# Depthwise convolution: the last terms of each channel tile as matrix products with diagonals

## The chip, the cores and the metric

The kernel runs on one core of one Trainium2 chip. Its time is the device time of one execution in microseconds (us). Three executions of the kernel before took 3126.61, 3127.12 and 3130.42 us; the median, 3127.12, is the time before. The engines are PE (TensorE, the matrix engine), DVE (VectorE), ACT (ScalarE), POOL (GpSimd) and SP (SyncE, which here issues the weight transfers). SBUF is the on-chip memory that all of them read, PSUM the memory into which PE writes its sums, in eight banks of 512 float32 for each of 128 partitions.

## The reference, cut to what matters

Two blocks run one after the other on 256 tokens of width 1024, all in float32. The second block also carries 256 context tokens, so its first layer works on 512 columns. In that first layer, between two feed-forward parts, stands the module that the change touches:

```
def conformer_conv(h, pw1_w, pw1_b, dw_w, dw_b, ln_g, ln_b, pw2_w, pw2_b):
    a = h @ pw1_w + pw1_b
    u, g = jnp.split(a, 2, axis=-1)
    u = u * jax.nn.sigmoid(g)
    u = lax.conv_general_dilated(            # depthwise, width 31, centred
        u, dw_w[:, None, :], window_strides=(1,), padding=[(15, 15)],
        feature_group_count=D_MODEL) + dw_b
    mu = jnp.mean(u, axis=-1, keepdims=True)
    var = jnp.mean(jnp.square(u - mu), axis=-1, keepdims=True)
    u = (u - mu) * lax.rsqrt(var + NORM_EPS) * ln_g + ln_b
    return jax.nn.silu(u) @ pw2_w + pw2_b
```

It is applied to the latent tokens and to the context tokens apart. The second layer has an attention in its place. Each layer is steered by nine vectors (shift, scale and gate of three parts), `silu(c) @ ada_w + ada_b`: a product of two rows with a matrix of 1024 x 9216.

## The kernel before, in words

**Layout.** Channels lie on the partitions, 128 at a time: KT = 8 channel tiles. Tokens lie along the free dimension. In the second block's first layer a tile is 512 columns: two sequences of 256.

**Split products.** A float32 product is made of three fast ones. Both operands are split into a high part (rounded by ACT in a copy) and a low part (the rest, by DVE or POOL: `low = raw - high`). `mm3` multiplies low by high, high by low and high by high into one sum.

**The stream of weights.** All weights stand in HBM in the order of their use, cut into quarters of 128 x 512 float32 (256 KB). `stream()` lists them. SP loads them in that order into a ring of RING = 11 places (`raw`). A place is free again when the quarter 11 before has been split (its low part is done) or, for an unsplit quarter, when PE has used it. ACT makes the high parts (`high`, L1277), and mostly DVE the low parts (`low`, L1720).

**Fills.** The steering products are done in 36 "fills" strewn over the kernel: one fill is eight unsplit quarters, multiplied with the two rows `cs` (`ps<-raw,cs`, 16 instructions on PE). Afterwards ACT copies the result (`row_buf`), PE turns it into columns (`ps<-cst,row_buf`) at the start of the next fill, and DVE takes the columns (`mods_raw`, then `mods` and `mod_a`). 18 fills stand in the conv stage: two for each channel tile and two behind. LATE_FILLS = 3 stand in the attention of the second layer, between its projections and its scores, in front of one more that PE does behind the scores.

**The conv stage** (`conv` of each engine). For channel tile n, PE computes the two halves of the first pointwise product into the banks 2(n%2) and 2(n%2)+1: four quarters, in two halves of 24 matmuls, with a fill behind each. ACT takes the sigmoid of one bank (`gated<-ps,cst`), and DVE multiplies and writes the result to `conv_in` (`hidden<-ps,cst,gated`: "the gate"; `conv_in`, `conv_out` and `side` are all pieces of the buffer `hidden` and bear its name in the trace). PE may write a pair of banks again when the gate two tiles before is done.

Then come the 31 terms. A term is `sum = conv_in[shifted by t] * w[t] + sum` over 128 x 512, one instruction (scalar_tensor_tensor, L1723). Each waits for the one before (`link`), since it reads its sum. DVE keeps the running sum `acc` in PSUM, bank 4 + n%2; only the last term writes to `conv_out` in SBUF. The first SIDES[n] terms of tile n = 1 to 7 are not done by DVE: ACT multiplies (`hidden<-hidden,cst` on ACT, into one of four buffers `side`) and POOL adds them up in `conv_out` (L2304 for the first, L2306 for the others). DVE waits for their sum and starts from it, so its first term of such a tile reads `conv_in` and `conv_out` and writes PSUM (`ps<-hidden,cst`), its middle ones read `conv_in` and PSUM (`ps<-hidden,cst,ps`), and the last reads the same and writes `conv_out` (`hidden<-hidden,cst,ps`).

The order within each engine is written out by hand. DVE takes the gate of tile n+2 near the end of tile n. POOL makes the low parts of the weight quarters from tile 1 on (L2276), two of them between the first side sums of each tile and two at its end. ACT makes the high parts at fixed places between its side products.

When all eight tiles are summed, PE forms the mean, DVE subtracts it, PE forms the variance, and norm, silu and the second pointwise product follow.

## Time and profile before

| | before |
|---|---|
| device time, median of 3 | 3127.12 us (3126.61 to 3130.42) |
| span of the profiled execution, first to last instruction | 3127.4 us |
| PE busy | 2965.4 us, 95% |
| DVE busy | 1637.2 us, 52% |
| ACT busy | 1291.8 us, 41% |
| POOL busy | 167.0 us, 5% |
| weights moved | 443.10 MB in all, 142 GB/s over the span |

The span of the profiled execution and the times of the others agree to 0.1%. Shares are means over stages with different limits. The profile also cuts the span into 40 slices of 78 us and gives the busy share of each engine in tenths:

```profile
PE   7999899999998999999999878999999999989998
DVE  5565765555647656533335796433335333448554
ACT  4444445455544455432332444323324323335553
POOL 0000010000010100000000670000000000000000
```

The conv stage is where POOL has its 6 and 7. Names such as `ps<-hidden,cst,ps` say what an instruction writes and reads: `ps` is PSUM, `hidden` and all others are SBUF. `cst` holds constants, here the weight w[t] of a term, one value for each partition. 128x512 is partitions times elements. The text in brackets at the end of a row is the idle time of the engine before it, and who ended it.

### The profile page before, as it was taken

The numbers are of one execution on the slowest core, as the hardware profiler recorded it, in microseconds if no ns is written. First come the engines' busy times: TensorE is split into PE (matmuls) and PEld (weight loads), VectorE is DVE, ScalarE is ACT, GpSimd is POOL, SyncE is SP. The second block draws the span as 40 slices with busy tenths as digits, with TensorE's granted clock in tenths as the row PEclk, the third lists the DMA queues.
The fourth block names the chain that finished last, engine by engine and source line by source line (L and its number), as shares of the span: only waits on it lengthen the run. The fifth ranks groups of instructions, "written<-read, shape, count | busy, mean of one in ns | idle before, by whom it ended". The sixth has DMA issues, their size and how long they took to land.

```text
span 3127.4 us, 51125 instructions
## 1 busy us (share of the span) xinstructions
PE 2965.4 (95%) x17586; PEld 2533.1 (81%) x17586; DVE 1637.2 (52%) x3043; ACT 1291.8 (41%) x2519; POOL 167.0 (5%) x121
## 2 busy tenths in 40 slices
PE   7999899999998999999999878999999999989998
PEld 7978789799797897788886545788878888768998
DVE  5565765555647656533335796433335333448554
ACT  4444445455544455432332444323324323335553
POOL 0000010000010100000000670000000000000000
PEclk9999899999998999999999988999999999989999
DMA  7555265555652656533333762333314233241553
GB/s 256 184 163 199 72 202 178 174 183 182 181 161 69 220 179 177 172 108 95 104 97 114 256 223 81 121 95 96 105 54 139 92 106 98 81 143 50 175 181 98
DMA packets 239052, 443.10 MB, mean 142 GB/s; under 512 B 26400, under 2 KB 27424, under 8 KB 238240
## 3 DMA queue, kind: packets, MB, share of 16 engines
q1 hardware_dynamic: 237344, 432.94, 44.1%
q0 software_dynamic: 1536, 7.86, 0.8%
q8 instruction: 108, 1.77, 0.2%
q14 instruction: 64, 0.52, 0.1%
HBM read 439.65 MB, written 1.05 MB: 141 GB/s over the span
## 4 chain that ended last, share of the span: by engine, by line
PE 82%; DVE 12%; issue 2%; POOL 2%; ACT 1%; DMA 1%; SPq 0%; DVEq 0%; POOLq 0%; ACTq 0%
PE ps L736 81%; DVE low L1720 1%; DVE hidden L1723 1%; POOL hidden L2306 1%; DVE zl L1723 1%; DMA raw<-weights 1%; DVE ps L1723 1%; DVE hidden L1720 1%; DVE zl L1720 1%; DVE coef L2228 1%; DVE hidden L2232 1%; POOL low L2276 1%; DVE gated L1720 1%; DVE hidden L2055 0%; DVE neg_max L2028 0%
## 5 line engine op out<-in xcount | busy, mean ns | idle before, releaser
L736 PE MATMUL ps<-zh,low 128*128 128x256 f32 (+1 forms) x4192 | 1400.6, 334 | 79.1 <-DVE low L1720 41.1
L736 PE MATMUL ps<-zl,high 128*128 128x256 f32 (+1 forms) x4192 | 1381.8, 330 | 0.0
L736 PE MATMUL ps<-zh,high 128*128 128x256 f32 (+1 forms) x4192 | 1380.9, 329 | 0.0
L1720 DVE TENSOR_TENSOR low<-raw,high 128x512 fp32r<-128x512 f32 x1276 | 843.8, 699 | 462.1 <-ACT high L1277 460.3
L1277 ACT ACTIVATE high<-raw 128x512 fp32r<-128x512 f32 x1304 | 761.7, 625 | 572.6 <-PE ps L736 499.5
L736 PEld LDWEIGHTS ps<-zh,low 128*128 128x128 f32 x4192 | 806.0, 192 | 184.0 <-DVE low L1720 42.2
L736 PEld LDWEIGHTS ps<-zl,high 128*128 128x128 f32 x4192 | 806.7, 192 | 71.8 <-issue 4.8
L736 PEld LDWEIGHTS ps<-zh,high 128*128 128x128 f32 x4192 | 806.5, 192 | 69.1
L1720 DVE TENSOR_TENSOR hidden<-gated,ps 128x256 f32 (+1 forms) x176 | 91.5, 520 | 604.2 <-ACT gated L1277 604.2
L1277 ACT ACTIVATE gated<-ps 128x256 f32<-128x256 f32 (+1 forms) x176 | 81.3, 462 | 497.3 <-PE ps L736 497.1
L736 PE MATMUL ps<-high,zl 128*128 128x512 f32 (+2 forms) x544 | 195.2, 359 | 3.8 <-DVE zl L1720 3.8
L736 PE MATMUL ps<-low,zh 128*128 128x512 f32 (+2 forms) x544 | 195.0, 359 | 0.0
L736 PE MATMUL ps<-high,zh 128*128 128x512 f32 (+2 forms) x544 | 195.0, 358 | 0.0
L1723 DVE SCALAR_TENSOR_TENSOR ps<-hidden,cst,ps 128x512 f32<-128x512 f32 x167 | 126.1, 755 | 5.4
L736 PEld LDWEIGHTS ps<-high,zl 128*128 128x128 f32 x544 | 103.1, 189 | 19.4 <-DVE zl L1720 4.3
L736 PEld LDWEIGHTS ps<-high,zh 128*128 128x128 f32 x544 | 103.2, 190 | 15.2
L736 PEld LDWEIGHTS ps<-low,zh 128*128 128x128 f32 x544 | 103.2, 190 | 15.1
L1277 ACT ACT_TABLE_LOAD x61 | 78.3, 1283 | 84.8 <-PE ps L736 83.0
L1277 ACT ACTIVATE zh<-hidden 128x256 fp32r<-128x256 f32 (+1 forms) x190 | 94.6, 506 | 45.0 <-DVE hidden L1720 28.4
L1720 DVE TENSOR_TENSOR zl<-hidden,zh 128x256 fp32r<-128x256 f32 (+1 forms) x190 | 101.3, 545 | 2.0 <-ACT zh L1277 1.9
L1723 DVE SCALAR_TENSOR_TENSOR x<-ps,mods,x 128x256 f32<-128x256 f32 x80 | 35.0, 479 | 126.3 <-PE ps L736 126.3
L1277 ACT ACTIVATE hidden<-ps,neg_max 128x128 f32<-128x128 f32 (+2 forms) x128 | 61.5, 484 | 81.0 <-DVE neg_max L2028 49.3
(190 smaller groups left out, 2016.8 us busy)
## 6 DMA issues: line engine op xcount, KB each, us to landing
raw<-weights SPq DMA_DIRECT2D x1640, 256.0 KB, 3.4
hidden<-norms POOLq DMA_DIRECT2D x4, 1024.0 KB, 7.0
cst<-consts SPq DMA_DIRECT2D x1, 1829.0 KB, 14.3
x<-x_in SPq DMA_DIRECT2D x1, 1024.0 KB, 7.0
x<-tokens_in POOLq DMA_DIRECT2D x1, 1024.0 KB, 13.8
x<-ctx_in POOLq DMA_DIRECT2D x1, 1024.0 KB, 6.4
out<-hidden POOLq DMA_DIRECT2D x1, 1024.0 KB, 5.1
ple_p<-p_in POOLq DMA_DIRECT2D x1, 512.0 KB, 7.2
```

Source lines behind the costliest of these rows:

```text
L736: return nc.tensor.matmul(out, lhsT, rhs, start=first, stop=last, **kw)
L1277: return nc.scalar.activation(out, in_, func, **kw)
L1720: return nc.vector.tensor_tensor(out, a, b, op)
L1723: return nc.vector.scalar_tensor_tensor(out, a, s, b, op0, op1)
L2228: self.link(nc.vector.tensor_reduce(coef[:, j, 0:1], ps[:, score_bank(j), :], AX.X, ALU.max))
L2232: nc.vector.tensor_copy(probs_t[:, b, :], ps[:, 3 + b, :]).then_inc(probs_t_ready, 1)
L2276: nc.gpsimd.tensor_tensor(r(low[:, q % RING, :]), raw[:, q % RING, :], high[:, q % RING, :], ALU.subtract).then_inc(low_ready, 1)
L2306: nc.gpsimd.tensor_tensor(part, part, side[:, at % 4, :], ALU.add).then_inc(side_added, 1)
```

## The change

- The last 4 terms of the tiles 0 to 6 and the last 12 of tile 7 (TAP_QUARTERS) are done by PE. For each term the weight is a 128 x 128 diagonal matrix; four of them make a quarter, and ten such quarters are added to the stream. ACT makes the high and POOL the low part, as of other weights. `tap_product` multiplies them with shifted views of a window of `conv_in`: `window_of` on ACT writes its high part, `window_of` on DVE its low part, into a buffer `split_buf` that is also the old `h_split`. The sum stands in bank 4 + n%2, and DVE adds it (`add_taps`), which ends a tile.
- DVE's running sum moves from PSUM to `conv_out` in SBUF for all its terms.
- SIDES shrinks from (0, 7, 9, 9, 9, 9, 9, 13) to (0, 3, 6, 7, 7, 7, 7, 4): 41 instead of 65 terms by way of ACT and POOL.
- The eight quarters of tiles 0 and 1 have no fill between them, and DVE makes their low parts ahead of the stage. The conv stage has 15 fills instead of 18, and LATE_FILLS is 6 instead of 3.
- POOL makes the low parts from tile 2 on and those of the ten diagonal quarters: 34 instead of 28.
- The gate of tile n+1 is taken in the middle of tile n instead of the gate of n+2 near its end.

```diff
-SIDES = (0, 7, 9, 9, 9, 9, 9, 13)
-LATE_FILLS = 3
+SIDES = (0, 3, 6, 7, 7, 7, 7, 4)
+TAP_QUARTERS = (1, 1, 1, 1, 1, 1, 1, 3)
+LATE_FILLS = 6
+WINDOW = 268
+def conv_fill(n, a):
+    return n >= 2 or (n, a) == (1, 1)
+def taps_by_pe(n):
+    return 4 * TAP_QUARTERS[n]
@@ stream, the conv part
             for t in range(KT):
                 for a in range(2):
                     yield ("up_half", ("conv", 0), (t, a), 2, False)
-                    yield fills.pop()
-            yield fills.pop()
-            yield fills.pop()
+                    if conv_fill(t, a):
+                        yield fills.pop()
+                if t >= 2:
+                    yield ("taps", ("conv", 0), t - 2, TAP_QUARTERS[t - 2], False)
+            for t in (KT - 2, KT - 1):
+                yield ("taps", ("conv", 0), t, TAP_QUARTERS[t], False)
+                yield fills.pop()
@@ class PE
+            def tap_product(self, n, z0):
+                self.pe.wait_ge(tap_low, n + 1)
+                if n >= 2:
+                    self.pe.wait_ge(z_ready, z0 + n - 1)
+                last = taps_by_pe(n) - 1
+                for c0 in range(0, last, 4):
+                    h, lo = self.quarter()
+                    for i in range(4):
+                        at = slice(c0 + i, c0 + i + S)
+                        w = (h[:, i * P:i * P + P], lo[:, i * P:i * P + P])
+                        m = self.mm3(ps[:, 4 + n % 2, :], w, (window[:, n % 2, 0, :, at], window[:, n % 2, 1, :, at]), c0 + i == 0, c0 + i == last)
+                    self.done(m)
@@ class PE, conv
                     for a in range(2):
...
-                        self.fill(6, 7)
+                        if conv_fill(n, a):
+                            self.fill(6, 7)
+                    if n >= 2:
+                        self.tap_product(n - 2, z0)
                 seen(conv_taken, KT)
-                self.fill(6, 7)
-                self.fill(6, 7)
+                for n in (KT - 2, KT - 1):
+                    self.tap_product(n, z0)
+                    self.fill(6, 7)
@@ class Act
+            def window_of(self, n):
+                self.act.wait_ge(conv_taken, self.seen.now(conv_taken) + n + 1)
...
+                self.f(r(window[:, n % 2, 0, :, 0:wide]), conv_in[:, n, :, at:at + wide], ACT.Copy).then_inc(tap_high, 1)
@@ class Act, conv, at the end of a tile's side products
                     if n < KT - 1:
-                        self.q += 2
                         self.gate_of(n + 1)
-                        self.fill(6, 7)
-                    if n < KT - 2:
+                        filled()
                         self.next_high()
                         self.next_high()
+                        self.take_rows()
+                        self.window_of(n + 1)
@@ class Dve, conv
+                def window_of(n):
+                    wide, at = S + taps_by_pe(n) - 1, TAPS - taps_by_pe(n)
+                    v.wait_ge(tap_high, n + 1)
+                    self.tt(r(window[:, n % 2, 1, :, 0:wide]), conv_in[:, n, :, at:at + wide], window[:, n % 2, 0, :, 0:wide], ALU.subtract).then_inc(tap_low, 1)
+                def add_taps(n):
+                    v.wait_ge(quarter_done, taps_at[n] + TAP_QUARTERS[n] + RING)
+                    self.tt(conv_out[:, n, :], conv_out[:, n, :], ps[:, 4 + n % 2, :], ALU.add).then_inc(z_ready, 1)
                 for n in range(KT):
-                    acc = ps[:, 4 + n % 2, :].rearrange("p (a s) -> p a s", a=2)
                     part = conv_out[:, n, :].rearrange("p (a s) -> p a s", a=2)
-                    for t in range(first, TAPS):
-                        last = t == TAPS - 1
-                        i = self.stt(part if last else acc, conv_in[:, n, :, t:t + S], w[:, n, t:t + 1], part if n and t == first else acc, ALU.mult, ALU.add)
...
+                    for t in range(first, last + 1):
+                        self.link(self.stt(part, conv_in[:, n, :, t:t + S], w[:, n, t:t + 1], part, ALU.mult, ALU.add))
...
+                            if t == first + 8:
+                                next_gate(n + 1)
+                                self.take_cols(7)
+                            if t == first + 12:
+                                window_of(n + 1)
+                        if t == first + (13 if n < KT - 1 else 4):
+                            add_taps(n - 1)
...
+                add_taps(KT - 1)
@@ gpsimd, the conv loop
-                    if t in (1, 2) and n < KT - 1:
-                        low_of(n + 1, 1 + t)
-                if n < KT - 2:
-                    low_of(n + 2, 0)
-                    low_of(n + 2, 1)
+                    if t in (1, 2) or t == SIDES[n] - 1 and n < KT - 1:
+                        next_low()
+                    if t == SIDES[n] - 1 == 2:
+                        next_low()
+                if n < KT - 1:
+                    next_low()
+                    next_low()
```

On DVE, a tile in the middle of the conv stage reads before, from the first term of tile 3 to that of tile 4 (`ps<-hidden,cst` is a first term, `hidden<-ps,cst,gated` a gate):

```order
L1723 SCALAR_TENSOR_TENSOR ps<-hidden,cst 128x512
L1723 SCALAR_TENSOR_TENSOR ps<-hidden,cst,ps 128x512 x6
L1788 COPY mods_raw<-ps 128x8
L1723 SCALAR_TENSOR_TENSOR ps<-hidden,cst,ps 128x512 x10
L1723 SCALAR_TENSOR_TENSOR hidden<-ps,cst,gated 128x2x256
L1723 SCALAR_TENSOR_TENSOR ps<-hidden,cst,ps 128x512 x2
L1788 COPY mods_raw<-ps 128x8
L1720 TENSOR_TENSOR mods<-mods_raw,cst 128x16
L1723 SCALAR_TENSOR_TENSOR mod_a<-mods,cst 128x16
L1723 SCALAR_TENSOR_TENSOR ps<-hidden,cst,ps 128x512 x2
L1723 SCALAR_TENSOR_TENSOR hidden<-hidden,cst,ps 128x512
```

And now, a round of the same kind, from one gate to the next (`split_buf<-hidden,split_buf` is the low part of a window, `hidden<-hidden,ps` the sum of the taps):

```order
L1788 SCALAR_TENSOR_TENSOR hidden<-ps,cst,gated 128x2x256
L1853 COPY mods_raw<-ps 128x8
L1788 SCALAR_TENSOR_TENSOR hidden<-hidden,cst 128x512 x4
L1785 TENSOR_TENSOR split_buf<-hidden,split_buf 128x2x259
L1788 SCALAR_TENSOR_TENSOR hidden<-hidden,cst 128x512
L1785 TENSOR_TENSOR hidden<-hidden,ps 128x512
L1788 SCALAR_TENSOR_TENSOR hidden<-hidden,cst 128x512 x8
L1853 COPY mods_raw<-ps 128x8
L1785 TENSOR_TENSOR mods<-mods_raw,cst 128x16
L1791 TENSOR_SCALAR mods<-mods 128x16
L1788 SCALAR_TENSOR_TENSOR hidden<-hidden,cst 128x512 x7
```

22 terms with the sum in PSUM, but for the first, have become 20 with the sum in SBUF, and a window and a tap sum stand between them.

On POOL, one tile reads before (L2276 makes a low part, L2304 and L2306 add side terms):

```order
L2304 TENSOR_SCALAR hidden<-hidden,cst 128x512
L2306 TENSOR_TENSOR hidden<-hidden 128x512
L2276 TENSOR_TENSOR low<-raw,high 128x512
L2306 TENSOR_TENSOR hidden<-hidden 128x512
L2276 TENSOR_TENSOR low<-raw,high 128x512
L2306 TENSOR_TENSOR hidden<-hidden 128x512 x6
L2276 TENSOR_TENSOR low<-raw,high 128x512 x2
```

And now:

```order
L2364 TENSOR_SCALAR hidden<-hidden,cst 128x512
L2366 TENSOR_TENSOR hidden<-hidden 128x512
L2338 TENSOR_TENSOR low<-raw,high 128x512
L2366 TENSOR_TENSOR hidden<-hidden 128x512
L2338 TENSOR_TENSOR low<-raw,high 128x512
L2366 TENSOR_TENSOR hidden<-hidden 128x512 x4
L2338 TENSOR_TENSOR low<-raw,high 128x512 x3
```

Two side sums fewer and one low part more: 12 instructions for a tile instead of 13.

## Rows read from the trace of the kernel before

**Rows 1.** Table of stretches: busy time by engine, clock, transfers
```profile
core 0: us, PE busy (x) PEld busy (x) DVE busy (x) ACT busy (x) POOL busy (x), PEclk, DMA share, GB/s
1682.60:1894.99 212.39, 164.53 (x831) 104.83 (x829) 167.48 (x269) 87.42 (x145) 120.66 (x93) 0.91 0.65 219
```

**Rows 2.** Groups of DVE, 1703.8 to 1895: busy, mean ns, idle before
```profile
line engine op names shapes xcount | busy us, mean ns | idle before us <-releasers
L1723 DVE SCALAR_TENSOR_TENSOR ps<-hidden,cst,ps 128x512 f32<-128x512 f32 x167 | 126.1, 755 | 5.4
L1723 DVE SCALAR_TENSOR_TENSOR ps<-hidden,cst 128x512 f32<-128x512 f32 x7 | 6.8, 969 | 6.0 <-POOL hidden L2306 6.0
L1723 DVE SCALAR_TENSOR_TENSOR hidden<-ps,cst,gated 128x512 f32<-128x512 f32 x7 | 5.3, 752 | 19.7 <-ACT gated L1277 19.7
```

**Rows 3.** DVE in order of time, conv stage: start, length, instruction, idle before
```profile
1707.27 8.66 DVE L1723 SCALAR_TENSOR_TENSOR ps<-hidden,cst,ps 128x512 f32<-128x512 f32 x11
...
1851.14 0.75 DVE L1723 SCALAR_TENSOR_TENSOR hidden<-ps,cst,gated 128x512 f32<-128x512 f32 x1
...
1894.32 0.75 DVE L1723 SCALAR_TENSOR_TENSOR hidden<-hidden,cst,ps 128x512 f32<-128x512 f32 x1
1897.31 4.61 DVE L1720 TENSOR_TENSOR hidden<-hidden,ps 128x1024 f32<-128x1024 f32 x4 [1.04 <-PE ps L736]
```

**Rows 4.** The ring of weight quarters on PE and ACT, by time
```profile
1746.63 1.92 PE L736 MATMUL ps<-raw,cs 128*32 128x512 f32 x16
1756.71 0.63 ACT L1277 ACTIVATE high<-raw 128x512 fp32r<-128x512 f32 x1 [6.79 <-DMA raw<-weights]
1761.22 0.50 PE L736 MATMUL ps<-zh,low 128*128 128x512 f32 x1 [1.52 <-POOL low L2276]
```

**Rows 5.** The head of the conv stage, by time
```profile
1692.83 0.48 DVE L1723 SCALAR_TENSOR_TENSOR zl<-hidden,mods,zh 128x256 fp32r<-128x256 f32 x1 [0.18 <-ACT zh L1277]
1694.05 1.28 DVE L1720 TENSOR_TENSOR low<-raw,high 128x512 fp32r<-128x512 f32 x2
1702.96 0.75 DVE L1723 SCALAR_TENSOR_TENSOR hidden<-ps,cst,gated 128x512 f32<-128x512 f32 x1 [7.63 <-ACT gated L1277]
```

**Rows 6.** Terms with two operands in SBUF, and POOL beside them
```profile
1836.53 1.28 POOL L2306 TENSOR_TENSOR hidden<-hidden 128x512 f32<-128x512 f32 x1
1837.02 1.35 DVE L1723 SCALAR_TENSOR_TENSOR ps<-hidden,cst 128x512 f32<-128x512 f32 x1
1856.04 1.66 DVE L1723 SCALAR_TENSOR_TENSOR ps<-hidden,cst 128x512 f32<-128x512 f32 x1
1769.86 2.50 POOL L2276 TENSOR_TENSOR low<-raw,high 128x512 fp32r<-128x512 f32 x2
```

**Rows 7.** POOL's first sums by source line: least, median, longest ns
```profile
L2304 POOL TENSOR_SCALAR hidden<-hidden,cst x7: 1561/1566/2071, 1727.3 to 1852.7; 128x512 f32<-128x512 f32 x7
```

**Rows 8.** POOL's norm products alone, and beside DVE's splits
```profile
232.07 4.79 POOL L2286 TENSOR_TENSOR x<-x,hidden 128x1024 f32<-128x1024 f32 x2
1066.45 5.62 POOL L2286 TENSOR_TENSOR x<-x,hidden 128x1024 f32<-128x1024 f32 x2
1061.77 10.86 DVE L1720 TENSOR_TENSOR low<-raw,high 128x512 fp32r<-128x512 f32 x4
```

**Rows 9.** PE by time: first and last of 19 matmuls of a product
```profile
1709.19 0.39 PE L736 MATMUL ps<-zh,high 128*128 128x512 f32 x1
...
1713.28 0.39 PE L736 MATMUL ps<-zh,high 128*128 128x512 f32 x1
```

**Rows 10.** The late fills of attention by time
```profile
2794.66 3.70 DVE L1720 TENSOR_TENSOR zl<-hidden,zh 128x512 fp32r<-128x512 f32 x6
2798.49 1.87 PE L736 MATMUL ps<-cst,row_buf 128*128 128x2 f32 x8 [8.14 <-DVE mods_raw L1788]
2804.82 1.02 PE L736 MATMUL ps<-cst,row_buf 128*128 128x2 f32 x8 [0.89 <-ACT row_buf L1277]
2810.58 0.50 PE L736 MATMUL ps<-zh 64*128 64x512 f32 x2 [0.69 <-ACT row_buf L1277]
```

**Rows 11.** Table of stretches behind the last late fill's start
```profile
2806.00:2810.00 4.00, 3.89 (x16) 0.63 (x8) 0.39 (x3) 0.07 (x1) 0.00 (x0) 1.00 1.01 363
2810.00:2814.00 4.00, 2.96 (x19) 1.93 (x20) 2.10 (x5) 3.00 (x6) 0.00 (x0) 1.00 1.05 393
```

More of the change, by code:

```diff
@@ L444, in build @@
         side_before = [sum(SIDES[:n]) for n in range(KT)]
+        up_at, taps_at, fill_at = {}, {}, []
+        at = 0
+        for kind, key, t, n, _ in stream():
+            if kind == "up_half":
+                up_at[t] = at
+            elif kind == "taps":
+                taps_at[t] = at
+            elif kind == "ada" and up_at:
+                fill_at.append(at)
+            if key == ("pw2", 0):
+                break
+            at += n
+        pw2_at = at
         q_at = carve(0, KT, S)
@@ L2265, in _, with next_low @@
             pool.dma_start(x[:, :, S:512], tokens_in).then_inc(tokens_landed, 16)
-            first = 0
-            for kind, key, _, n, _ in stream():
-                if key == ("conv", 0):
-                    break
-                first += n
-            starts = [first + (2 + KT) * h for h in range(2 * KT)]
-            def low_of(n, i):
-                q = starts[2 * n + i // 2] + i % 2
+            coming = iter([q for q in range(up_at[2, 0], pw2_at) if not RAW[q]])
+            def next_low():
+                q = next(coming)
                 pool.wait_ge(high_ready, sum(not a for a in RAW[:q + 1]))
@@ L2289, in _ @@
             pool.dma_start(x[:, :, S:512], ctx_in).then_inc(ctx_landed, 16)
[L2291 to L2295 removed]
+            pool.wait_ge(low_ready, sum(not a for a in RAW[:up_at[2, 0]]))
+            next_low()
+            next_low()
             for n in range(1, KT):
```

112 lines of the change are left out of this document (54 added, 58 removed).

## The prediction

> **What bounds the kernel now.** The engine shares of the page come first: PE is busy for 95% of the span, but the slices show a hole at slices 20 to 24, the only ones in which POOL works. That is the conv stage, 1682.6 to 1895, and a table of stretches shows PE at 165 of its 212 us there [rows 1]. So in this stage something else ends last. The groups of DVE instructions in the stage show what [rows 2]: from the first gate to the last term DVE has 183 convolution terms, 7 more gates and some small work, and its main idle times are 19.7 us before gates and 6.0 before POOL's last side sum. The terms are linked, each waits for the one before: 11 took 8.66 us, 0.79 each [rows 3]. The last one ends at 1895.0 [rows 3], and only then can the statistics, the norm and the second pointwise product follow. DVE's string of terms is the bound, and close beside it a ring of transfers: a fill ends at 1748.5, ACT gets the next weight quarter at 1756.7 after a wait of 6.8 us, POOL splits two quarters with a side sum between, and PE starts at 1761.2 [rows 4]. That is 8.2 us behind the fill for the transfers, 4.5 for the splits, and with a product (5.1) and a fill (2.9) the ring turns in about 20.7 us; the gates are 21.2 us apart (seven from 1703.0 to 1851.1, rows 3 and 5).
>
> **The change, part by part.**
>
> *The head.* The eight quarters of tiles 0 and 1 now stand without a fill between them, and DVE splits all eight before the gate. Now the last zl ends at 1693.3, two splits follow (1.28), PE's second half product waits for them, and DVE starts its gate at 1702.96 [rows 5]. Afterwards four more splits at 0.64 stand ahead of the last zl, 2.6 us: it ends near 1695.8, the product some 1 us later, the sigmoid (0.69) near 1697.5. DVE's gate starts at 1697.7 and ends at 1698.5, 5.2 us earlier than before.
>
> *DVE's own time from there.* Terms: 27+24+21+4x20+15 = 167 (4 to 12 go to PE, and the side terms shrink from 65 to 41, which gives DVE back 24 of the 40 that PE takes). 167 x 0.79 = 131.9. Seven gates 5.5. Eight low windows of 518 columns at the price of a 512 split, 0.65: 5.2. Eight sums from PSUM at half of a 1024 one (4.61 for four, rows 3), 0.6: 4.9. 15 column copies and 13 small operations at 0.2: 5.6. Sum 153.1. The same count for before is 156.3, so by instruction time alone nearly nothing is gained: 16 terms go, 16 window and sum operations come.
>
> *Where the sum of a term is kept.* This decides. Before, the running sum is in PSUM, and a term reads one operand from SBUF. PE's tap products now need those banks, so the running sum moves to `conv_out` in SBUF, and 166 terms and 8 windows read two operands from SBUF. The trace of before has exactly this instruction seven times, at the first term of each tile (`ps<-hidden,cst`). Beside a side sum of POOL it took 1.35, where it takes 0.75: POOL's sum ended at 1837.81 and the term 0.56 later [rows 6]. Another beside POOL took 1.66. The other five took 0.75, four of them beside POOL's one-operand TENSOR_SCALAR; but one of these POOL instructions took 2.07 instead of 1.56, so it gave way [rows 7]. The mean of the seven is 969 ns against 755 for the form with the sum in PSUM [rows 2]. The cleanest place is at 1061: four splits of DVE (0.64 each elsewhere) took 10.86, while two of POOL's norm products beside them took 5.62 against 4.79 when alone [rows 8]. So the two alternate: POOL pays about 0.42 for each of the two DVE instructions that it lets in, and DVE waits out each POOL instruction.
>
> A round of one POOL instruction and one term is thus 1.25 (two splits in 2.50, rows 6) + 0.50 (the 0.42 of a split and the 0.51 of the 2.07) = 1.76 instead of 0.79: 0.97 more on DVE for each POOL instruction. POOL has 34 splits (28 before), 34 side sums and 7 first sums: 75. 75 x 0.97 = 73. What runs beside the gates, PSUM sums and copies (0.79+0.6+0.4 per tile) costs less; POOL works about half of the time, so I take off 8: **+65**. Bounds: nothing (all land beside DVE's other work), and 75 x 1.25 = 94 if DVE waits for every one in full.
>
> The Trainium skill (SBUF — State Buffer, Who interferes with whom) has the rule: a VectorE instruction with two SBUF inputs contends with a GpSimd instruction that reads SBUF, and the one that comes first keeps the shared pair for its whole time. The trace agrees in kind; in size, full blocking would make a round 2.0 (1.25+0.75), 1.21 more each, and the end 19 us later than my sum. The rows show a cheaper round.
>
> End of the terms: 1698.5 + 153.1 + 65 = 1916.6, against 1895.0: **+21.6**. Behind it the path to the second product stays as it is.
>
> *What hides beside this.* A tile now takes DVE about 29 us. PE has per tile two products of 24 at 0.227 [rows 9], two fills at 2.9 (turning the rows 1.0, rows 10; weights 1.92, rows 4) and 12 tap matmuls at 0.227: 19.4. The ring needs 20.7. ACT's windows and the split quarters of the diagonals lie in the slack of 8 us. Cover gone (rival 1), they would bind. The last 36 tap matmuls (8.2 us, 16 at the low clock) start about 10 us after the last gate, and DVE ends about 30 after it; at the low clock the fill and the statistics behind could end some us later than DVE. I cost it at nothing and keep 5 for the range.
>
> *The three fills that leave the stage.* LATE_FILLS goes from 3 to 6. In the conv stage their absence gains nothing, since PE waits there. In attention they stand ahead of the scores, whose operands are ready at 2798.4, when DVE has ended the sixth zl [rows 10]. PE runs two of the three fills behind that point, at 2798.5 and 2804.8, and starts the scores at 2810.6. From the third fill on the transfers run without a break, at 363 and then 393 GB/s [rows 11]. Each further fill needs eight quarters, 2.1 MB, at a mean of 378: 5.5 us. Three: **+16.6**. Bounds: 11 if only PE and the row copy counted (2.9+0.9 each), 18 at the pace of the last fill (2804.82 to 2810.58 is 5.8). The skill's page on SBUF (Two separate sides) gives about 436 GB/s as the peak of the transfers; by that the three would cost 14.4. The rows are nearer.
>
> Sum: 3127.4 + 21.6 + 16.6 = 3165.6. The profiled execution (3127.4) agrees with the median of the runs, 3127.1, so nothing is corrected: **3166**.
>
> **Rivals.**
>
> 1. *The terms do not meet POOL (faster).* If the sums in SBUF cost 0.75 as in five of the seven rows, the ring of transfers decides from the third gate on. Gate 2 near 1727, five turns of 20.7 give gate 7 at 1830. The quarter with the first diagonal of tile 7 lands 8.2 us behind the fill there (1840), and ACT waits for it ahead of the window, which DVE needs: window 1842, 7 terms and a sum, then 15 terms and a sum: about 1862. That is -33, with the fills +16.6: 3111. For it: the kernel's end of the terms is long now, 44 us behind gate 7. Against it: rows 6 and 8. It decides from a price under 0.35 us per POOL instruction on. Chance 0.09.
>
> 2. *Full blocking.* 1.21 per POOL instruction, or POOL's work all inside the terms: +84 to +94 instead of +65: 3185 to 3195. For it: the row of 1.66. Against it: POOL paid only 0.42 per pass in rows 8. Chance 0.14.
>
> 3. *Half.* POOL's first sums (7) do not block, splits fall beside gates, and the price is 0.5: +37, so -6 in conv and +16.6: 3138. For it: four one-operand rows. Chance 0.09.
>
> **How the numbers follow.** Forecast 0.68, rivals 0.09, 0.14, 0.09. About 0.2%, 6 us, is what a measurement of this kernel can tell from no change. The forecast's own range is 3152 to 3180 (price 0.8 to 1.1, late tail of PE 5, fills 11 to 18). Leaving out rival 1 and the ends of 2 and 3 gives 3144 to 3188. Faster 0.09, same 0.03, slower 0.88.
>
> **What would show it.** The terms as `hidden<-hidden,cst` should have a mean of 1.1 to 1.2 us in place of 0.755, bimodal between 0.75 and 1.9; POOL's back-to-back splits should be 1.7 apart. Gates should be 28 to 30 us apart, with DVE hardly idle and PE waiting for DVE and POOL. The last term should end near 1917. In attention the scores should start 16 to 17 us after the point where they start now, behind fills that wait for weights. I am wrong if the terms stay at 0.75 to 0.8 (then 3111), or if the gates come at 20.7 with ACT waiting for weights.

## The result, and the profile after

The changed kernel takes 3194.32 us (median of 4, 3191.68 to 3195.99), the kernel before, run beside it, 3127.22. The ratio is 1.0214, with a 95% interval of 1.0200 to 1.0228. It is slower, as forecast, but by 67 us instead of 39, and lies outside the range of 3144 to 3188. The profiled execution has a span of 3190.9, 63.5 more than before.

Where these 63.5 lie can be read from one kind of instruction that both kernels run 36 times: ACT's copies of a fill's rows (`row_buf`), which mark the stages; they are counted from 0 here. Between two marks stands:

| stretch of the program | before | after | difference |
|---|---|---|---|
| start to copy 9 (at 1301.0 before) | 1301.0 | 1300.1 | -0.9 |
| feed-forward part ahead of the conv stage (copy 9 to 10) | 375.7 | 384.4 | +8.7 |
| conv stage, norm and second product | 294.0 | 314.8 | +20.8 |
| second feed-forward part | 375.8 | 384.8 | +9.0 |
| third feed-forward part | 376.1 | 384.5 | +8.4 |
| projections of attention | 73.1 | 72.1 | -1.0 |
| late fills, to the last copy | 14.2 | 34.7 | +20.5 |
| the rest | | | -2.1 |

The conv stage came out as forecast (+20.8 against +21.6), the late fills a little dearer (+20.5 against +16.6). The 26 us of the three feed-forward parts stood nowhere in the prediction: the change does not touch a line of them.

**The conv stage.** DVE's groups in the stage of the changed kernel answer to [rows 2]: count, busy time, mean ns of one, idle time before them and who ended it.

```profile
line engine op names shapes xcount | busy us, mean ns | idle before us <-releasers
L1788 DVE SCALAR_TENSOR_TENSOR hidden<-hidden,cst 128x512 f32<-128x512 f32 x166 | 174.7, 1053 | 12.5 <-POOL hidden L2366 7.8
L1785 DVE TENSOR_TENSOR split_buf<-hidden,split_buf 128x518 fp32r<-128x518 f32 (+1 forms) x8 | 7.6, 953 | 4.5 <-ACT split_buf L1335 4.3
L1788 DVE SCALAR_TENSOR_TENSOR hidden<-ps,cst,gated 128x512 f32<-128x512 f32 x8 | 6.0, 752 | 1.0 <-ACT gated L1335 0.7
L1785 DVE TENSOR_TENSOR hidden<-hidden,ps 128x512 f32<-128x512 f32 x8 | 5.5, 687 | 0.3
```

A term has become `hidden<-hidden,cst` and takes 1053 ns on average instead of 755. The waits for gates, 19.7 us before, have gone to 1.0: DVE is the bound, as forecast. POOL's groups in the same stretch:

```profile
L2366 POOL TENSOR_TENSOR hidden<-hidden 128x512 f32<-128x512 f32 x34 | 53.3, 1568 | 3.0
L2338 POOL TENSOR_TENSOR low<-raw,high 128x512 fp32r<-128x512 f32 x34 | 52.9, 1562 | 489.7 <-ACT high L1335 489.7
```

Both forms took 1.28 to 1.29 before. Terms and POOL slow each other down, and in order of time DVE's rows around the gate of tile 5 show how unevenly (they answer to [rows 3] and [rows 6]; start, length, instruction). The last row is POOL's, from the same moments:

```profile
1834.66 0.75 DVE L1788 SCALAR_TENSOR_TENSOR hidden<-ps,cst,gated 128x512 f32<-128x512 f32 x1
...
1839.59 1.79 DVE L1788 SCALAR_TENSOR_TENSOR hidden<-hidden,cst 128x512 f32<-128x512 f32 x1
1841.42 0.69 DVE L1785 TENSOR_TENSOR hidden<-hidden,ps 128x512 f32<-128x512 f32 x1
1842.02 9.52 DVE L1788 SCALAR_TENSOR_TENSOR hidden<-hidden,cst 128x512 f32<-128x512 f32 x6
1852.76 2.43 DVE L1788 SCALAR_TENSOR_TENSOR hidden<-hidden,cst 128x512 f32<-128x512 f32 x2 [1.22 <-POOL hidden L2366]
...
1915.57 7.83 DVE L1788 SCALAR_TENSOR_TENSOR hidden<-hidden,cst 128x512 f32<-128x512 f32 x10
1923.43 0.69 DVE L1785 TENSOR_TENSOR hidden<-hidden,ps 128x512 f32<-128x512 f32 x1
...
1845.85 6.81 POOL L2366 TENSOR_TENSOR hidden<-hidden 128x512 f32<-128x512 f32 x4
```

Six terms beside POOL take 9.52, 1.59 each, while four of POOL's sums take 6.81, 1.70 each; the ten terms from 1915.57 on, when POOL has ended, take 0.78 each. From tile 2 to tile 7 the gates are 27.6 to 30.2 us apart, as the prediction's signs had it; the mean of the terms lies below its 1.1 to 1.2. The last sum ends at 1924.1, 29 us later than before [rows 3]; 7.8 of this were there when the stage began.

**The late fills.** PE in order of time, the multiplication of the second late fill, then a later one whole and the next turn of rows (compare [rows 10]), and then a table of the stretch (us, busy time of PE, PEld, DVE, ACT and POOL, granted clock, transfer share, GB/s; compare [rows 11]):

```profile
2845.41 3.64 PE L775 MATMUL ps<-raw,cs 128*32 128x512 f32 x16
...
2856.46 1.84 PE L775 MATMUL ps<-cst,row_buf 128*128 128x2 f32 x8 [0.78 <-ACT row_buf L1335]
2858.23 4.26 PE L775 MATMUL ps<-raw,cs 128*32 128x512 f32 x16
2863.27 1.84 PE L775 MATMUL ps<-cst,row_buf 128*128 128x2 f32 x8 [0.78 <-ACT row_buf L1335]
```

```profile
2850.00:2856.00 6.00, 5.69 (x24) 2.56 (x24) 0.17 (x1) 0.28 (x1) 0.00 (x0) 0.50 0.97 319
2856.00:2862.00 6.00, 5.54 (x24) 2.60 (x24) 0.34 (x2) 0.32 (x1) 0.00 (x0) 0.50 0.93 307
```

A fill takes 1.84 + 4.2 + 0.8 for the copy of its rows: 6.6 us in the mean of four (2849.19 to 2875.56). The granted clock is 0.50, PE's lower level of 1.2 GHz, and the transfers run at 307 to 319 GB/s, not at 378. At this level PE's own work with the row copy comes to 1.84 + 3.64 + 0.8 = 6.3 us already; the prediction had counted 3.8 for it. Three further fills at 6.6 are 19.8; the rest of the 20.5 is that the third fill, which the kernel before has too, took 5.9 there and takes 6.5.

**The feed-forward parts.** The same 80 us of PE's 512-column products, first in the kernel before, then in the changed one, both at full clock and without an idle moment (columns as in [rows 1]; the count behind PE's busy time is that of its matmuls):

```profile
2100.00:2180.00 80.00, 80.00 (x354) 66.25 (x353) 24.61 (x39) 22.65 (x40) 0.00 (x0) 1.00 0.33 101
```

```profile
2100.00:2180.00 80.00, 80.00 (x346) 64.87 (x345) 23.41 (x37) 22.61 (x38) 0.00 (x0) 1.00 0.31 100
```

354 matmuls against 346, 2.3% fewer: one every 231 ns instead of 226. No wait has been added; the matmuls themselves are slower. Not all of them, though. In the whole first part (PE's groups, 1300 to 1684 in the changed kernel) those that stream zh have gone from 389 to 395 ns, as have those that stream zl; those that stream `split_buf` are at 390, where they were at 389:

```profile
L775 PE MATMUL ps<-zh,high 128*128 128x512 f32 x512 | 202.1, 395 | 0.0
L775 PE MATMUL ps<-split_buf,high 128*128 128x512 f32 x32 | 9.9, 390 | 0.0
```

Products of 256 columns have not become slower: 671 of them in 1100 to 1180 against 669 before. What the change did touch is an allocation: `split_buf` has 4 x 2 x 268 = 2144 floats in each partition, where `h_split` had 2 x 2 x 512 = 2048.

### The profile page after: what moved, and what is told of

It is laid out like the page before. It is cut to its first block, busy times and chain, and to the rows that moved or that the text cites. A ratio compares the mean times of both kernels' runs of the same rounds, so it can differ in the third digit from the quotient of the medians.

```text
span 3190.9 us, 51371 instructions
## 1 busy us (share of the span) xinstructions
PE 3030.7 (95%) x17706; PEld 2555.0 (80%) x17706; DVE 1683.2 (53%) x3047; ACT 1285.1 (40%) x2513; POOL 163.9 (5%) x103
## 4 chain that ended last, share of the span: by engine, by line
PE 81%; DVE 13%; POOL 2%; issue 1%; ACT 1%; DMA 1%; SPq 0%; DVEq 0%; ACTq 0%; POOLq 0%
PE ps L775 81%; DVE hidden L1788 4%; DVE low L1785 2%; POOL hidden L2366 1%; DMA raw<-weights 1%; DVE zl L1788 1%; DVE hidden L1785 1%; DVE x L1791 1%; DVE zl L1785 1%; DVE coef L2295 1%; DVE hidden L2299 1%; DVE hidden L2120 0%; DVE neg_max L2093 0%; ACT hidden L1335 0%; DVE gated L1785 0%
## 5 line engine op out<-in xcount | busy, mean ns | idle before, releaser
L775 PEld LDWEIGHTS ps<-zh,low 128*128 128x128 f32 x4192 | 797.1, 190 | 172.4 <-DVE low L1785 35.2
L775 PEld LDWEIGHTS ps<-zl,high 128*128 128x128 f32 x4192 | 797.4, 190 | 80.0 <-issue 4.8
L775 PEld LDWEIGHTS ps<-zh,high 128*128 128x128 f32 x4192 | 797.0, 190 | 77.8
L1788 DVE SCALAR_TENSOR_TENSOR hidden<-hidden,cst 128x512 f32<-128x512 f32 x166 | 174.7, 1053 | 12.5 <-POOL hidden L2366 7.8
```

What stands on the lines that cost most here:

```text
L775: return nc.tensor.matmul(out, lhsT, rhs, start=first, stop=last, **kw)
L1788: return nc.vector.scalar_tensor_tensor(out, a, s, b, op0, op1)
```

## The experiments

They ran in four batches, each beside the kernel before on the same chip (3125.41, 3126.25, 3127.09 and 3127.87); ratios are to it, with their 95% interval.

### Whose 26 us: the addresses of what PE streams

`split_buf` is longer by 96 floats in each partition (384 bytes) and stands in front of x, zh and zl, which start 384 bytes later. Theory: PE streams zh and zl more slowly from there. **pad96_before** is the kernel before with one more line:

```diff
         h_split = sb("h_split", [P, 2, 2, 512])
+        pad = sb("pad", [P, 96])
         x = sb("x", [P, KT, 512])
```

> The kernel before, with nothing but an unused tensor of 96 float32 (384 bytes) per partition allocated in front of x, zh and zl, as the longer split_buf of the changed kernel shifts them. Theory A (the shift slows PE where it reads 512 columns): the three 512-column feed-forward parts take 8 to 9 us longer each, as in the changed kernel (row copy 9 to 10: 375.7 before, 384.4 after), and the second pointwise product 1 to 2 us: 3152 to 3157. Theory B (something else in the changed program slows these stages, such as its length or its order): 3127, no change. Matmuls of 512 columns start 0.2267 us apart under B, 0.231 to 0.233 under A.

Measured: 3149.36, ratio 1.0067 (1.0045 to 1.0088). The parts take 384.5 each, and PE's row is that of the changed kernel:

```profile
2100.00:2180.00 80.00, 80.00 (x346) 64.85 (x345) 22.82 (x36) 22.44 (x38) 0.00 (x0) 1.00 0.30 95
```

An unused buffer alone makes the loss. **moved_after** goes the other way: the changed kernel with `split_buf` allocated behind zl.

> The changed kernel, with split_buf allocated behind zl, so that x, zh and zl start at a multiple of 2048 bytes behind where they stood before. Theory A (address): the 512-column stages are back at the pace of before, 26 to 28 us less than the changed kernel: 3166 to 3169. Theory B (not the address): 3194. The conv stage and the attention do not change under either: the last term ends 21 to 22 us later than before, counted from the start of the stage.

Measured: 3168.09, ratio 1.0129 (1.0106 to 1.0151). The first part takes 375.6 again, and the conv stage and the late fills keep their losses. This is what the prediction was about, and 3166 would have been right for it: by the marks its conv stage costs 20.1 more than before and its late fills 20.1.

Which buffer, and which shift, was asked with the same line in other places and sizes: **pad96_behind** (behind zl), **pad96_x_zh** (between x and zh), and in front of x with 16, 64 and 128 floats (**pad16_before**, **pad64_before**, **pad128_before**).

> The kernel before with an unused SBUF tensor of 96 floats allocated behind zl instead of in front of x, so that x, zh and zl stand where they stood, and only the smaller buffers behind are shifted by 384 bytes. Theory (PE's 512-column matmuls lose 2.3% when zh and zl, which they stream, are shifted): row copy 10 stands 375.7 us behind row copy 9 as in the kernel before, time 3125 to 3128. Rival (any shift or any added length does it, or the shift of the constants, which lie behind as well): 384.5 and 3149.

> The kernel before with the 96 floats between x and zh: x stays, zh and zl are shifted by 384 bytes. Theory (what counts is what PE streams, zh and zl): 384.5 per 512-column stage and 3149, as with the tensor in front of x. Rival (x counts, which DVE and ACT work on, or the distance between x and zh): 375.7 and 3125 to 3128.

> The kernel before with an unused SBUF tensor of 16 floats (64 bytes) in front of x, so that x, zh and zl start 64 bytes behind a multiple of 2048. Theory A (a 512-column row that PE streams must not cross a 2 KB boundary, or must start on one): the 512-column stages take 384.5 as with 96 floats, 3149. Theory B (the cost grows with the shift, or starts from a coarser step): between 375.7 and 378, 3125 to 3132.

> The kernel before with 64 floats (256 bytes) in front of x. So far, matmuls of 512 columns in 80 us at full clock: 354 without a shift and at 512 bytes, 351 to 352 at 64 bytes, 346 at 384 bytes. Theory C (a 512-column row whose start is not at a multiple of 512 bytes costs, in a size that goes with the remainder): at 256 bytes between these, 348 to 349, 381 to 382 us per stage, time 3138 to 3145. Rival (only 256 bytes count, and 384 is bad as 128 behind such a step): 354, and 3125 to 3128.

> The same with 128 floats (512 bytes). Theory A (start on 2048): 384.5 and 3149. Theory B (a finer alignment, of 512 bytes, is enough): 375.7 and 3125 to 3128. pad96 was 384 bytes, which is no multiple of 512.

| kernel | shift of zh, zl | matmuls in 1400:1480, 2100:2180, 2500:2580 | ratio (95% interval) |
|---|---|---|---|
| before | 0 | 354, 354, 355 | |
| pad16_before | 64 B | 352, 351, 351 | 0.9984 (0.9968 to 1.0001) |
| pad64_before | 256 B | 354, 354, 355 | 1.0004 (0.9992 to 1.0015) |
| pad96_before | 384 B | 346, 346, 346 | 1.0067 (1.0045 to 1.0088) |
| pad96_x_zh | 384 B | 344, 346, 346 | 1.0085 (1.0068 to 1.0102) |
| pad128_before | 512 B | 355, 354, 354 | 0.9999 (0.9985 to 1.0012) |
| pad96_behind | 0 | 355, 355, 355 | 1.0007 (0.9997 to 1.0017) |

The rows behind the table, pad16_before's, pad96_x_zh's and pad64_before's:

```profile
2100.00:2180.00 80.00, 80.00 (x351) 65.64 (x350) 22.82 (x36) 21.72 (x38) 0.00 (x0) 1.00 0.31 97
```

```profile
2100.00:2180.00 80.00, 80.00 (x346) 64.88 (x345) 22.12 (x35) 21.99 (x37) 0.00 (x0) 1.00 0.31 95
```

```profile
2100.00:2180.00 80.00, 80.00 (x354) 66.28 (x353) 22.82 (x36) 21.74 (x38) 0.00 (x0) 1.00 0.32 98
```

It is zh and zl that count, not x and not what stands behind; the two were always shifted together. Two of my theories fell: a start at 2048 is not needed (pad128_before), nor one at 512 (pad64_before). What the runs show: 0, 256 and 512 bytes cost nothing, 64 bytes 0.9% and 384 bytes 2.3%. A multiple of 256 fits all five, but no other shift was tried, and why some shifts cost PE time and others not stays open. pad16_before lost 3.3 us in each feed-forward part, between the two figures that I had put down for it, and was no slower in all: it was 7.3 us ahead at copy 9, and 3.8 of these it had gained between the marks at 1046 and 1248, where DVE's splits and POOL's norm products meet [rows 8]. Such small gains and losses change with any edit, and a difference of 5 us in a total says little by itself here; the count of matmuls says it plainly.

**aligned512_after** is the changed kernel with 32 unused floats behind `split_buf`: a shift of 512 bytes.

> The changed kernel with 32 unused floats behind split_buf, so that x, zh and zl are shifted by 512 bytes against the kernel before instead of by 384. Theory (a multiple of 512 bytes is enough): 375.7 per 512-column stage, and the time of the changed kernel with split_buf behind zl, 3166 to 3170. Rival (in the changed kernel the loss comes from a shift of any size against split_buf): 384.5 and 3194.

Measured: 3161.02, ratio 1.0100 (1.0083 to 1.0117), and the feed-forward parts at 375.7 to 376.1:

```profile
2100.00:2180.00 80.00, 80.00 (x354) 66.24 (x354) 22.17 (x36) 22.76 (x39) 0.00 (x0) 1.00 0.30 94
```

With 128 bytes of nothing in each partition the changed kernel is 33 us faster; 26 of these lie in the three feed-forward parts. Another 3.5 lie in the late fills, in the last four of which PE here had its full clock, and the rest in stretches whose times differ by as much between other kernels.

### The sum in SBUF

**sbuf_sum_before** does this part of the change alone:

```diff
-                    acc = ps[:, 4 + n % 2, :].rearrange("p (a s) -> p a s", a=2)
-                    part = conv_out[:, n, :].rearrange("p (a s) -> p a s", a=2)
+                    part = acc = conv_out[:, n, :].rearrange("p (a s) -> p a s", a=2)
```

> The kernel before with one part of the change alone: the running sum of DVE's terms is kept in conv_out (SBUF) instead of in PSUM; nothing else differs. Theory (contention for SBUF between DVE's terms with two SBUF inputs and POOL): POOL has 93 instructions in the stage (28 splits, 58 side sums, 7 first sums), and in the changed kernel each of 75 cost DVE about 0.66 us (166 terms at 1.053 instead of 0.755). So the terms should have a mean near 1.10 us, POOL's passes 1.56 instead of 1.28, and the conv stage should be 93 x 0.66 = 61 us longer: 3187, between 3175 and 3200. Rival: the sum in SBUF costs nothing by itself, and the longer terms of the changed kernel come from its windows and quarters: 3125 to 3130. Second rival, DVE waits for every POOL instruction in full, 93 x 1.25 = 116: 3241.

Measured: 3181.59, ratio 1.0183 (1.0164 to 1.0203). DVE's terms and POOL's side sums in the stage:

```profile
L1723 DVE SCALAR_TENSOR_TENSOR hidden<-hidden,cst 128x512 f32<-128x512 f32 x182 | 209.2, 1152 | 11.6 <-POOL hidden L2305 6.0
```

```profile
L2305 POOL TENSOR_TENSOR hidden<-hidden 128x512 f32<-128x512 f32 x58 | 91.2, 1572 | 22.0 <-ACT hidden L1277 15.3 <-POOL hidden L2305 0.5
```

One operand moved, not one instruction more, and the kernel loses 55 us. 182 terms cost 0.40 more each, 72 us; part of it goes into what had been idle. For 93 POOL instructions that is 0.78 each on DVE and 0.56 in the stage's length (52 us from copy 10 to copy 29), where full waiting for each would give 116.

**psum_sum** does the opposite: moved_after with DVE's sum in PSUM again, in bank 4 alone, and PE's tap products in bank 5.

```diff
@@ PE.tap_product: it also waits for the tap sum of the tile before
-                if n >= 2:
-                    self.pe.wait_ge(z_ready, z0 + n - 1)
+                if n >= 1:
+                    self.pe.wait_ge(z_ready, z0 + n)
@@ Dve.conv: the sum
+                    acc = ps[:, 4, :].rearrange("p (a s) -> p a s", a=2)
...
-                        self.link(self.stt(part, conv_in[:, n, :, t:t + S], w[:, n, t:t + 1], part, ALU.mult, ALU.add))
+                        self.link(self.stt(part if t == last else acc, conv_in[:, n, :, t:t + S], w[:, n, t:t + 1], part if n and t == first else acc, ALU.mult, ALU.add))
```

> As moved_after, and DVE's running sum is back in PSUM (bank 4); the taps of PE have bank 5 alone, so a tap product waits for the tap sum of the tile before. Theory A (terms with two SBUF operands alternate with POOL, 0.97 us per POOL instruction, 65 us in all): the terms return to 0.755 us, and the ring of weight quarters (20.7 us a tile) bounds the stage: 50 to 60 us less than moved_after, 3106 to 3117. Theory B (POOL's neighbourhood costs little and DVE's string is long for another reason): at most 10 us less, 3156 or more.

Measured: 3150.96, ratio 1.0080 (1.0058 to 1.0102): 17 us less than moved_after, where I had expected 50 to 60. Its groups:

```profile
L1788 DVE SCALAR_TENSOR_TENSOR ps<-hidden,cst,ps 128x512 f32<-128x512 f32 x149 | 112.4, 754 | 4.3
...
L1788 DVE SCALAR_TENSOR_TENSOR ps<-hidden,cst 128x512 f32<-128x512 f32 x7 | 5.9, 847 | 29.7 <-POOL hidden L2367 29.7
```

```profile
L2367 POOL TENSOR_TENSOR hidden<-hidden 128x512 f32<-128x512 f32 x34 | 43.8, 1288 | 3.0
```

The contention is gone on both sides (754 and 1288 ns). But DVE now stands idle for 29.7 us before the first terms of tiles. The gates are 24 to 27 us apart, not 20.7, and the stage ends 5.9 us later than before instead of some 30 earlier. **psum_gate_early** asked whether the place of the gate does it:

```diff
-                            if t == first + 8:
+                            if t == first + 3:
                                 next_gate(n + 1)
                                 self.take_cols(7)
-                            if t == first + 12:
+                            if t == first + 8:
                                 window_of(n + 1)
```

> psum_sum (the change with DVE's running sum back in PSUM), with the gate of tile n+1 behind DVE's 3rd term of tile n instead of its 8th, and its low window behind the 8th instead of the 12th. The question is where psum_sum's gain went: its DVE stands idle for 30 us before tile starts. Theory: its tiles turn in a ring of waits: gate (1831.57) -> high window on ACT (1832.36) -> side products, with ACT waiting for a diagonal's quarter among them -> POOL's last side sum (about 1847) -> DVE's first terms of the next tile -> its gate 8 terms later. Taking the gate 5 terms (4 us) earlier shortens each of the six turns by up to 4 us: about 20 us less than psum_sum's 3151, so 3128 to 3136, unless transfers then hold it. Rival (ACT's waits for weight transfers, 72 us in psum_sum, set the pace, not the gate's place): 3146 to 3152, with gates still 24 to 26 apart.

Measured: 3156.01, ratio 1.0089 (1.0072 to 1.0106). My theory fell: the gates still come 23 to 26 us apart (1728.68, 1751.96, 1778.21, 1804.14, 1829.04, 1854.84), and what DVE no longer waits for POOL it waits for ACT's window (20.9 us). The two kernels' waits in the stage name what both share; these two are psum_sum's (total, times, longest):

```profile
ACT high L1335 <- DMA raw<-weights: 72.3, 14, 11.0
...
DVE mods_raw L1853 <- PE ps L775: 11.6, 1, 11.6
```

From 1807.84 to 1831.63 psum_sum's PE runs through one tile: it is busy for 19.9 us (two products, two fills, twelve tap matmuls), waits 1.5 for POOL's split of the quarter that came last and 2.3 for the column copy and the row copy. ACT, which does its work in order, makes that row copy at 1824.65, behind a wait of 5.9 us for a weight quarter. So the ring by way of PE, transfers, ACT and POOL turns in 24 us and not in 20.7. And at the end the three diagonal quarters of tile 7 hold PE until 1889.3 and with it DVE's column copy, 11.6 us. This is a reading of one trace: that the gate's place is not the cause was tested, the ring itself was not taken apart. Nor was the wait that psum_sum adds, a tap product's for the tap sum of the tile before.

### The price of a late fill

**late5_before** is the kernel before with two of the 18 fills of the conv stage moved into attention (LATE_FILLS = 5).

> The kernel before, with the two fills at the end of its conv stage moved to the attention (LATE_FILLS 5, conv stage 16). Theory A (each late fill costs its eight transfers): scores start 11 us later, and the 6 us of waiting for POOL's last side sum in the conv stage go away, since the row copy that held ACT up is gone: 3131 to 3138. Theory B (a late fill costs PE's time and the row copy, 3.8 us): 3129 to 3131 or 3135 without the gain in conv; scores 7.6 us later.

Measured: 3132.34, ratio 1.0014 (1.0001 to 1.0026). Between the marks the conv stage was 7.7 shorter (its last term ends at 1889.1 instead of 1895.1, and it began 1.7 later), and the two fills cost 13.9 in attention: 6.9 each. One of the late fills has a wait of 1.8 for a weight quarter inside, at full clock. **warm_moved** is moved_after with PE kept busy around the late fills:

```diff
+                self.stream(18)
                 for _ in range(LATE_FILLS):
                     self.fill(6, 7)
+                    self.stream(6)
```

> moved_after with PE kept busy around the late fills: 18 matmuls without use ahead of the first and 6 behind each. In the changed kernel PE stands at the low clock (0.50) in the whole of the late fills, a fill takes 1.84 + 4.0 + 0.8 for the row copy = 6.6 us, and the transfers run at 305 to 330 GB/s; in the kernel before the last fill ran at full clock with transfers at 364. Theory (the low clock is why a late fill costs 6.5 and not the forecast 5.5): the granted clock is 1.0 there, a fill takes 5.5 to 5.9, and the time falls by 3 to 5 us to 3163 to 3165. Rival (transfers set the pace in any case, and their rate varies): still 6.4 to 6.6 per fill, 3168 or more.

Measured: 3164.51, ratio 1.0112 (1.0096 to 1.0129). PE by time and two stretches:

```profile
2833.23 0.95 PE L775 MATMUL ps<-cst,row_buf 128*128 128x2 f32 x8
2834.11 4.21 PE L775 MATMUL ps<-raw,cs 128*32 128x512 f32 x16
```

```profile
2830.00:2836.00 6.00, 6.00 (x31) 2.84 (x29) 0.17 (x1) 0.60 (x1) 0.00 (x0) 1.00 0.90 298
2836.00:2842.00 6.00, 5.99 (x32) 2.81 (x30) 0.52 (x3) 0.60 (x1) 0.00 (x0) 1.00 1.01 380
```

At full clock the turn of rows takes 0.95 instead of 1.84, but the multiplication still 4.21 where its 16 matmuls need 1.92 [rows 4]: it now waits inside for quarters (from 2816 to 2846, 14 such waits, 6.9 us). Row copies come 6.04 us apart (2820.19 to 2844.36, four), against 6.5 in moved_after, and not the 5.5 to 5.9 that I had expected. The filled stretch shows that transfers alone, at 298 GB/s in one stretch and 380 in the next, hold a fill above 5.5. How much of the price is the low clock's, this run does not separate: moved_after, which it is compared with, was itself at the low clock only up to 2830, and its last three fills at full clock still took 6.6 each, with PE waiting for quarters. Over the runs, the changed kernel and psum_gate_early, low from the second late fill on, have 6.6 and 6.8 for a fill (the last four of each), and aligned512_after, at full clock from its third late fill on without any filler, 5.7.

### A version that beats both

In the kernel before, ACT has its last copy of rows in the stage in front of its last side product of tile 7; it waits there for PE's last fill, until 1877.8, and DVE then waits 6.0 for POOL [rows 2]. **rows_behind** changes one number:

```diff
-                            if t == 11:
+                            if t == 12:
                                 self.take_rows()
```

> The kernel before with ACT's last copy of a fill's rows in the conv stage behind its last side product of tile 7 instead of ahead of it. In the kernel before ACT stands at this copy from 1865 to 1877.8 (it waits for PE's last fill), the last side product follows, POOL's last sum ends at 1880.3, and DVE waits 6.0 us for it. Theory (this wait is the end of the stage): POOL ends near 1871.5, DVE does not wait, the last term ends 6.0 earlier and the time is 3119.5. Rival (another wait takes its place, as PE's statistics behind the last fill): 3122 to 3125.

Measured: 3119.70, ratio 0.9977 (0.9967 to 0.9986). ACT's copy waits as long, behind the product, and hurts nobody:

```profile
1860.50 0.72 ACT L1277 ACTIVATE hidden<-hidden,cst 128x512 f32<-128x512 f32 x1 [0.69 <-POOL hidden L2306]
1872.38 0.60 ACT L1277 ACTIVATE row_buf<-ps 128x512 f32<-128x512 f32 x1 [11.16 <-PE ps L736]
```

**early_fills** adds what the late fills suggest: two of the three go to the end of the conv stage, where PE and the transfers stand idle, the opposite of what the change does.

```diff
-LATE_FILLS = 3
+LATE_FILLS = 1
@@ stream
-            yield fills.pop()
-            yield fills.pop()
+            for _ in range(4):
+                yield fills.pop()
@@ Dve.conv: columns taken earlier in tiles 6 and 7, and the values that a fill now overwrites too soon copied
-n >= KT - 2 and t == TAPS - 4
+n >= KT - 2 and t in (first + (6 if n == KT - 2 else 2), TAPS - 4)
...
+                    if n == 2:
+                        self.link(nc.vector.tensor_copy(mod_kept[:], mods[:, 5]))
```

> The kernel before with rows_behind's edit, and two of the three late fills moved the other way than in the change: from the attention (LATE_FILLS = 1) to the end of the conv stage's tiles, where PE stands idle from 1860 to 1872 and from 1885 to 1895. DVE takes the columns of tiles 6 and 7 earlier, and the modulation values that the conv residual still needs are copied aside. Theory: -6.0 for the wait, and -2 x 6.4 for the late fills (the price found in late5_before), so 3125 - 19 = 3106. Rival: at the end of the conv stage the two fills (2.9 us each at full clock, 5 at the low one) push PE's statistics behind the last term, and their transfers the quarters of the second pointwise product: 3112 to 3120.

Measured: 3108.82, ratio 0.9946 (0.9929 to 0.9962). **early_fills15** also gives POOL 15 instead of 13 side terms of tile 7.

> early_fills with 15 instead of 13 side terms in tile 7. POOL ends its last sum near 1869 there, DVE needs it near 1872. Theory: two more side sums (2.6 us) fit in this slack, DVE has two terms less, -1.6 us: 3107. Rival: POOL's sum comes later than DVE's need, and gain and wait cancel: 3109.

Measured: 3105.02, ratio 0.9923 (0.9906 to 0.9939). PE at the end of its stage, with the last two of the four fills that now stand there, at 1871.28 and 1876.57, and DVE's change to tile 7 without a wait:

```profile
1871.28 3.44 PE L737 MATMUL ps<-raw,cs 128*32 128x512 f32 x16
1875.62 1.03 PE L737 MATMUL ps<-cst,row_buf 128*128 128x2 f32 x8 [0.89 <-ACT row_buf L1278]
1876.57 3.62 PE L737 MATMUL ps<-raw,cs 128*32 128x512 f32 x16
1880.12 7.13 PE L737 MATMUL ps<-hidden,cst 128*128 128x512 f32 x16
```

```profile
1871.88 0.75 DVE L1726 SCALAR_TENSOR_TENSOR hidden<-hidden,cst,ps 128x512 f32<-128x512 f32 x1
1872.54 0.75 DVE L1726 SCALAR_TENSOR_TENSOR ps<-hidden,cst 128x512 f32<-128x512 f32 x1
```

The last term ends at 1885.5 instead of 1895.1, and the fills cost the stage nothing. This version is 23 us faster than the kernel before and 89 faster than the changed one, and contains nothing of the change.

## Why the prediction was wrong

- **The step that failed** is the one that was not written down as a step: the sum has terms for the conv stage and for the late fills, and for the other 2800 us it says nothing, as if they could not change. The change's description has `split_buf` only as what PE's windows are kept in, and the prediction gives its length no term. This length shifted zh and zl, and that cost 26 us in the feed-forward parts. The profiled execution lies 25.3 above the sum: the 26.1 of these parts, 3.9 more for the late fills, 0.8 less for the conv stage, and 4.0 less in the stretches that were to stay as they were; that the last two of these nearly cancel the second is chance. With `split_buf` elsewhere the same kernel takes 3168.09 (moved_after).
- **The conv stage, +21.6: right, 20.8 by the marks.** The head: gate 0 at 1698.3 (7.8 us of delay from ahead of the stage taken off) against 1697.7. The last sum, by the same clock, at 1916.3 against 1916.6. That it is so close is partly luck: terms and windows cost 52 us in contention instead of 65 (terms at 1.053, below the 1.1 to 1.2 that I named), and 12 us of waits, 7.8 for POOL's side sums and 4.3 for ACT's windows, stand in for the rest, which I had at nothing.
- **A term and POOL: the mechanism right, its price between.** 0.97 per POOL instruction was too much; the changed kernel has 52 us for 75 of them, 0.69 each, and sbuf_sum_before gives 0.78 in DVE's busy time and 0.56 in the stage. The rule of the Trainium skill (SBUF — State Buffer, Who interferes with whom), that the loser stands still for the whole of the other's instruction, does not fit in size: where both engines work without a pause, a term takes 1.59 and a POOL sum 1.70, and one wholly behind the other would be 1.28 + 0.75 = 2.03. POOL's own instructions grew by 0.28 each (1568 against 1289 ns), and 93 full waits of DVE would have been 116 us, not 52. In its direction it holds: with the sum in PSUM both sides are back at 754 and 1288.
- **Late fills, +16.6: 20.5.** The size was off: 6.6 per fill instead of 5.5. I had taken the transfer rate from 8 us of one stretch in which PE was at full clock [rows 11]. In the changed kernel PE was at the low clock from the second of the six on, and there PE's own work with the row copy (6.3) nearly fills the time by itself; aligned512_after, at full clock, has 5.7.
- **Rival 1 (terms without contention), 3111,** assumed that the ring of transfers then turns in 20.7. psum_sum shows 24 to 27 without any contention: psum_sum's 3151 lies 40 above this rival, though psum_sum's tap products also wait for a sum that the rival's would not. The price of 0.35 below which this rival was to decide does not follow from its own terms: 1862 less 1698.5 and 153.1 leaves 10.4 us, 0.14 for each of 75 instructions. Nothing else rested on it. Rival 2 named the right size of the loss, 3185 to 3195, by a mechanism that sbuf_sum_before contradicts.

## What to carry to other kernels

When a change alters the size of a buffer, list what is allocated behind it and compare one stretch that the change does not touch, by its count of instructions in equal time, before explaining anything else; here 128 unused bytes in each partition were worth 26 us in three parts that nobody had touched. Before taking work off an engine that is the bound, see what the new work does to the others' operands: moving a running sum from PSUM to SBUF beside a busy POOL cost 55 us, more than the 16 terms fewer on DVE were worth (12.6 at 0.79 each). And ask where waits of in-order engines stand: one copy moved behind one product gave 0.2%, and two fills moved into a stretch in which PE and transfers idle another 0.3%.

## What the runs showed of the hardware that I had not expected

- Matmuls of 512 columns (float32 data in the one-pass form, at full clock) start every 226 ns with zh and zl at a shift of 0, 256 or 512 bytes, every 228 at 64 and every 231 at 384 bytes. Those of 256 columns show no such order: in 1100 to 1180 there are 671 in the changed kernel (384 bytes), 655 in pad96_before (384), 656 in aligned512_after (512) and 669 before. The Trainium skill (SBUF — State Buffer, Specifications) speaks of lines of 16 bytes; every shift tried is a multiple of 16, so this rule does not tell the cases apart.
- With PE kept busy its granted clock was 1.00 from 2824 on through the late fills (warm_moved), where the changed kernel had 0.50 in the same work, and a fill took 6.04 against 6.59. aligned512_after had 1.00 there without such help and took 5.71; what made its clock rise where the changed kernel's did not stays open.
